# A decoder step with 32 experts: three experts fixed by number, in blocks of 96 slots

## The chip, the core and the metric

The kernel runs on one core of a Trainium2 chip. The metric is the device time of one execution in microseconds (us); several executions are timed and their median is compared. The engines are called PE (TensorE), DVE (VectorE), ACT (ScalarE), POOL (GpSimd) and SP (SyncE, which here only issues transfers). PEld is the loading of PE's weights.

## What is computed

One step of a decoder layer in float32: a prompt of 1024 tokens and 8 sampled tokens, together 1032 rows of 1024 numbers. A gated convolution and latent attention are merged and normalised, and the result h goes through a mixture of 32 SwiGLU experts. This last part is the one that the change touches:

```python
grp = argmax(softmax(h @ router_w_group + b_group))            # 4 groups
le = (h @ router_w_expert + b_expert)[experts of grp]          # 8 in a group
top_l, top_i = top_k(le, 2)                                    # two experts a token
for each expert e, for its rows x:                             # 2064 rows in all
    hid = silu(x @ w_gate[e]) * (x @ w_up[e])                  # 1024 -> 512
    y[row] += weight * (hid @ w_down[e])                       # 512 -> 1024
out = layernorm(alpha * h + y)
```

Each expert has three matrices of 2 MB. By the reference's inputs the experts 0, 1 and 2 get 28, 25 and 26 rows; the fullest expert gets 111 and the emptiest 18.

## The kernel before

The attention part and the output projection run first (to about 1100 us of the span). Then the experts run one after another, 32 blocks, one for each expert. The program's order of blocks is fixed: block n is the expert of rank `RANK[n]`. The ranks are worked out on the chip: the experts are sorted by their count of rows (lines 1488 to 1505 on PE, 2502 to 2527 on DVE), except the first `FIXED` ones, which keep rank = number (`key_f`, line 2374, gives them a key above every count). The rank decides how many slots a block has (`full`, `three`, `low` and `room`, lines 514 to 524): 128, 96, 64 or 32. What an expert has above its slots would go to extra blocks at the end (`NOVER`, run only if counts demand them; in the profile none ran).

For block n PE does, in this order: `gate_up(n)` (gate and up products, line 1568), `rows_in(n+1)` (turning the gathered rows of the next block, line 1510), `down_proj(n-1)`, `turn_hidden(n)` (line 1535). A block of 128 slots makes gate first and then up, each over the whole array (line 1515; down at 1541). A block of 64 makes gate and up side by side in the two halves of the array (lines 1520, 1521; down 1547). A block of 32 uses four quarters (lines 1528, 1553). A block of 96 is a 32 and then a 64, and both its gate and its up are finished only at its end.

In block 0 the place of a down projection is taken by `slot_tables` (line 1562): it sums the lists of rows (`blk_tok`) and weights of all blocks out of one-hot products that DVE makes (`oh_w`, `oh_blk`, lines 2580 to 2583, signal `wt_rdy`). DVE's order is written out by hand, and those products stand behind `swiglu_gate(0)`, the multiplication of block 0's gate by its sigmoid. The first `SOON` = 2 blocks get their rows from an earlier, separate table (`first_tok`), so that they can start ahead of that.

SP loads the matrices into a ring of ten places (`ring_at`, `load_matrix`, line 759). Matrix j = 3 * expert block + (0 gate, 1 up, 2 down). The table `before` says whose place each takes; SP waits until that one has been multiplied (`g_done`, `u_done`, `d_done`). The places 8 and 9, which matrices 10 and 11 take, hold the one-hot products, so these two wait for the slot tables (`ws_dve`). Matrices 0 to 5 belong to the fixed experts 0 and 1 and are loaded before the ranks are known; from matrix 6 on SP first waits for `ord_dve`, the sorted order (line 782). SP's transfers are served in the order in which they are issued. POOL gathers the rows of a block (line 903) and adds its results to `sums` in memory (line 908).

```python
            for q in range(3):
                sp.wait_ge(h_out[q], H_BASE[q] + 16 * (NT // 3))
                sp.wait_ge(ah_out[q], A_BASE[q] + 16 * (NT // 3))
            sp.wait_ge(ord_dve, 1)
...
            for n in range(SOON, NE):
                e = expert_at(n)
                for m in range(3):
                    load_matrix(3 * n + m, e)
```

Of the kernel before, what the change touches and what calls it, by code (L numbers as in the profile page):

```python
# [15 lines left out]
ALU = mybir.AluOpType  # L16
# [25 lines left out]
NE = NG * EG  # L42
# [5 lines left out]
SOON = 2  # L48
# [16 lines left out]
class Chain:  # L65
# [5 lines left out]
    def link(self, ins):  # L71
        self.n += 1
        ins.then_inc(self.sem, 1)
        self.eng.wait_ge(self.sem, self.base + self.n)
# [11 lines left out]
def build(nc, a):  # L86
    ctx = ExitStack()
    with ctx:
        def sem(name):
            return ctx.enter_context(nc.semaphore(name))  # L90
# [317 lines left out]
        ord_dve = sem("ord_dve")  # L408
# [91 lines left out]
            p, rest = divmod(n + 1, 2 * NQ)  # L500
            return NQ * p + max(0, rest - NQ)

        FIXED, FULL, MID, LOW = 2, 10, 20, 30
        kinds = {"f": iter(range(FIXED, FULL)), "m": iter(range(FULL, MID)), "h": iter(range(MID, LOW)), "q": iter(range(LOW, NE))}
        RANK = list(range(FIXED)) + [next(kinds[c]) for c in "hhfmhfmhfmhmhfmhfmhfmhfmhmfmqq"]
        assert sorted(RANK) == list(range(NE))
        def main(n):
            return P if full(n) else P // 2
# [3 lines left out]
        assert T * NE < FIRST  # L512

        def full(n):
            return RANK[n] < FULL

        def three(n):
            return FULL <= RANK[n] < MID

        def room(n):  # L520
            return P if full(n) else 3 * P // 4 if three(n) else P // 4 if low(n) else P // 2

        def low(n):
            return RANK[n] >= LOW

        def rest(n):
            return low(n) or three(n)

        def rest_at(n):
            return P // 2 if three(n) else 0  # L530
# [9 lines left out]
        def place(j):  # L540
            return place_of[j]
# [59 lines left out]
        def _(sp):  # L601
# [156 lines left out]
            def load_matrix(j, e):  # L758

                if before[j] is not None:  # L760
                    n, m = divmod(before[j], 3)
                    sp.wait_ge((g_done, u_done, d_done)[m], n + 1)
                elif place(j) >= 8:
                    sp.wait_ge(ws_dve, 1)
                sp.dma_start(ring(j), matrix(j % 3, e)).then_inc(we_ld[place(j)], 16)
# [13 lines left out]
            for q in range(3):  # L779
                sp.wait_ge(h_out[q], H_BASE[q] + 16 * (NT // 3))  # L780
                sp.wait_ge(ah_out[q], A_BASE[q] + 16 * (NT // 3))
            sp.wait_ge(ord_dve, 1)

            def expert_at(n):
                return sp.value_load(order[0:1, RANK[n]:RANK[n] + 1].bitcast(I32), min_val=0, max_val=NE - 1)

            for n in range(SOON, NE):
                e = expert_at(n)
                for m in range(3):
                    load_matrix(3 * n + m, e)  # L790
            n, m = divmod(max(j for j in range(3 * NE) if place(j) == 6), 3)
# [35 lines left out]
        def _(pool):  # L827
# [72 lines left out]
            def gather_block(table, blk, par, loaded, rows=P):  # L900

                off = bass.IndirectOffsetOnAxis(ap=table[0:rows, blk:blk + 1].bitcast(U32), axis=0)
                pool.indirect_dma_start(xg[0:rows, par, :], None, h_rows, off, bounds_check=T - 1, oob_is_err=False).then_inc(loaded, 16)
# [14 lines left out]
            for e in range(NE + 4):  # L918
                if e < NE:
# [6 lines left out]
                    else:  # L926
                        gather_block(blk_tok, RANK[e], e % 2, xg_ld[e % 2], room(e))
                if e >= 4:
# [20 lines left out]
        def _(pe):  # L949
# [615 lines left out]
            def gate_up(n):  # L1565

                pe.wait_ge(we_ld[place(3 * n)], landed(3 * n))
                pe.wait_ge(te_act, n + 1)
                pe.wait_ge(te_dve, n + 1)
                pe.wait_ge(gm_dve, n)  # L1570
                if full(n):
                    up(2, ring(3 * n), n % 2).then_inc(g_done, 1)
                    pe.wait_ge(we_ld[place(3 * n + 1)], landed(3 * n + 1))
                    pe.wait_ge(hu_dve, n)
                    up(3, ring(3 * n + 1), n % 2).then_inc(u_done, 1)
                else:
                    pe.wait_ge(we_ld[place(3 * n + 1)], landed(3 * n + 1))
                    pe.wait_ge(hu_dve, n)
                    if rest(n):
                        g, u = up_rest(ring(3 * n), ring(3 * n + 1), n % 2, rest_at(n))  # L1580
                    if not low(n):
                        g, u = up_halves(ring(3 * n), ring(3 * n + 1), n % 2)
                    g.then_inc(g_done, 1)
                    u.then_inc(u_done, 1)
# [346 lines left out]
        def _(dve):  # L1931
            chain = Chain(dve, dve_chain)
            link = chain.link
            tt, stt = nc.vector.tensor_tensor, nc.vector.scalar_tensor_tensor
# [578 lines left out]
            def width(out, by):  # L2513

                link(ts(out, by, float(FULL), None, ALU.is_lt))
                link(stt(out=out, in0=by, scalar=float(MID), in1=out, op0=ALU.is_lt, op1=ALU.add))
                link(stt(out=out, in0=by, scalar=float(LOW), in1=out, op0=ALU.is_lt, op1=ALU.add))
                link(ts(out, out, float(P // 4), float(P // 4), ALU.mult, ALU.add))
# [203 lines left out]
```

## Time and profile before

| | us |
|---|---|
| median of 3 executions | 1719.39 |
| lowest, highest | 1716.16, 1719.78 |
| the profiled execution, its own time | 1711.8 |
| its span in the trace | 1710.0 |
| PE busy in the span | 1642.7 (96%) |
| DVE, ACT, POOL busy | 661.3, 339.4, 163.9 |

The span runs from the first to the last instruction; the profiled execution took 1.8 us more than its span, and 7.6 us less than the median. Starts in the trace are us from the start of the span. A group of instructions is called by its line in the kernel. The granted clock of PE is 1.00 at 2.4 GHz and 0.50 at 1.2 GHz. The DMA share is the mean busy share of the core's 16 DMA engines.

### The profile page before, as it was taken

To read this page: it belongs to the slowest core of one execution; us is meant where nothing else is said; L and a number is where in the kernel's file an instruction comes from. 1 tells how busy PE (TensorE), PEld (TensorE's weight loads), DVE (VectorE), ACT (ScalarE), POOL (GpSimd) and SP (SyncE) were. 2 spreads that over 40 slices of the span, in tenths; PEclk is the share of its full clock that TensorE was granted. 3 is DMA by queue.
4 is the path that set the end of the run, shared out by engine and by line. 5 is a ranking of instruction groups with operands and counts; after the bars stand their busy time and mean duration, and the time that the engine had idled before them with its cause. 6 is when DMAs were issued, how large, how long until landed. Compare 5 with 4: busy or idle time off the path is not lost.

```text
span 1710.0 us, 22521 instructions
## 1 busy us (share of the span) xinstructions
PE 1642.7 (96%) x9285; PEld 1009.8 (59%) x9286; DVE 661.3 (39%) x1395; ACT 339.4 (20%) x670; POOL 163.9 (10%) x169
## 2 busy tenths in 40 slices
PE   7999999999999999999999999999999999999990
PEld 5556777777777666666688555654444444444440
DVE  1446464544542323232477745551111212121225
ACT  1113222323231221222122000101111111111115
POOL 1000000000002422111000000001111111111110
PEclk9999999999999999999999999989999999999995
DMA  7201121121027445443263443289999999999975
GB/s 229 62 18 24 50 63 50 52 61 50 13 75 210 170 148 172 140 136 112 65 235 125 187 160 136 101 302 390 391 392 377 392 395 391 381 389 396 389 268 203
DMA packets 104410, 337.67 MB, mean 197 GB/s; under 512 B 24378, under 2 KB 68482, under 8 KB 87924
## 3 DMA queue, kind: packets, MB, share of 16 engines
q1 hardware_dynamic: 89572, 276.22, 43.0%
q0 software_dynamic: 13568, 55.78, 10.8%
q10 hardware_dynamic: 1168, 4.23, 0.6%
q8 instruction: 75, 1.23, 0.3%
q14 instruction: 27, 0.22, 0.0%
HBM read 307.90 MB, written 35.51 MB: 201 GB/s over the span
## 4 chain that ended last, share of the span: by engine, by line
PE 91%; DMA 5%; DVE 2%; issue 1%; ACT 1%; POOL 0%; SPq 0%; DVEq 0%; POOLq 0%; ACTq 0%
PE psum L1075 12%; PE psum L1189 10%; PE psum L1515 8%; PE psum L1520 7%; PE psum L1377 6%; PE psum L1392 5%; PE psum L1541 4%; PE psum L1116 4%; PE psum L1547 4%; PE psum L979 3%; PE psum L1228 3%; PE psum L1089 2%; DMA arena<-in_w_up 2%; PE psum L1134 2%; PE psum L1528 2%; PE psum L1123 2%
## 5 line engine op out<-in xcount | busy, mean ns | idle before, releaser
L1075 PE MATMUL psum<-arena 128*128 128x258 f32 x896 | 215.3, 384 | 0.0
L1189 PE MATMUL psum<-arena 128*128 128x344 f32 x576 | 182.3, 458 | 0.0
L1075 PEld LDWEIGHTS psum<-arena 128*128 128x128 f32 x896 | 162.9, 190 | 27.9 <-issue 7.0
L1520 PE MATMUL psum<-arena 128*64 128x512 f32 x320 | 141.6, 595 | 0.0
L1521 PE MATMUL psum<-arena 128*64 128x512 f32 x320 | 141.6, 595 | 0.0
L1515 PE MATMUL psum<-arena 128*128 128x512 f32 x320 | 139.8, 595 | 1.1 <-DVE arena L2552 1.1
L1189 PEld LDWEIGHTS psum<-arena 128*128 128x128 f32 x576 | 103.3, 190 | 52.9 <-issue 11.2
L1515 PEld LDWEIGHTS psum<-arena 128*128 128x128 f32 x320 | 60.0, 190 | 73.6 <-issue 73.2
L1377 PE MATMUL psum<-arena 128*128 128x258 f32 x448 | 99.9, 387 | 0.9 <-ACT arena L1802 0.9
L1392 PE MATMUL psum<-arena 128*128 128x512 f32 x224 | 99.2, 596 | 0.0
L1377 PEld LDWEIGHTS psum<-arena 128*128 128x128 f32 x448 | 86.6, 194 | 14.3 <-issue 1.3
L1520 PEld LDWEIGHTS psum<-arena 128*64 128x64 f32 x320 | 42.2, 137 | 85.0 <-issue 84.1
L872 POOL DMA_INDIRECT arena<-in_cache_ckv,arena x32 | 31.0, 968 | 620.4 <-DVE arena L2091 455.1
L2184 DVE COPY arena<-psum 128x512 f32<-128x512 f32 x64 | 44.2, 691 | 113.5 <-PE psum L1228 113.2
L1547 PE MATMUL psum<-arena 128*64 128x512 f32 x320 | 73.1, 598 | 0.0
L1116 PE MATMUL psum<-arena 96*128 96x512 f32 (+3 forms) x192 | 72.2, 488 | 0.0
L1541 PE MATMUL psum<-arena 128*128 128x512 f32 x160 | 71.3, 599 | 0.0
L1392 PEld LDWEIGHTS psum<-arena 128*128 128x128 f32 x224 | 41.5, 190 | 47.4 <-issue 47.3
L1228 PE MATMUL psum<-arena 128*128 128x128 f32 x512 | 66.3, 273 | 0.0
L1756 ACT COPY arena<-psum 128x512 f32<-128x512 f32 x64 | 37.5, 585 | 144.7 <-PE psum L1228 144.7
L908 POOL DMA_INDIRECT sums<-arena x32 | 47.7, 1491 | 191.3 <-DVE arena L2629 87.8
L1228 PEld LDWEIGHTS psum<-arena 128*128 128x128 f32 x512 | 59.2, 141 | 10.1 <-issue 0.2
(394 smaller groups left out, 2125.6 us busy)
## 6 DMA issues: line engine op xcount, KB each, us to landing
arena<-in_w_gate SPq DMA_DIRECT2D x32, 2048.0 KB, 24.7
arena<-in_w_up SPq DMA_DIRECT2D x32, 2048.0 KB, 30.3
arena<-in_w_down SPq DMA_DIRECT2D x32, 2048.0 KB, 30.6
arena<-in_w_in SPq DMA_DIRECT2D x33, 512.0 KB, 5.3
gates<-arena SPq DMA_DIRECT2D x16, 516.0 KB, 6.1
arena<-gates SPq DMA_DIRECT2D x16, 516.0 KB, 6.6
arena<-in_x_prompt SPq DMA_DIRECT2D x16, 512.0 KB, 4.5
arena<-in_w_o SPq DMA_DIRECT2D x1, 4096.0 KB, 17.6
```

The lines of the kernel that those rows point to most:

```text
L979: ins = mm(psum[0:m, 3 * s + b, 0:SP3], wring[:, slot, k, 0:m], xT[:, k, b * SP3:(b + 1) * SP3], start=(k == 0), stop=(k == KD - 1))
L1075: ins = mm(psum[:, BANK[name[0]], 0:QT], held, moved, start=(k == 0 and name in ("X1", "V6", "Y5")), stop=(k == 3), skip_group_check=True)
L1116: ins = mm(psum[:, 2 * hh + b // 512, 0:w], qT[0:QK, hh, i * P:(i + 1) * P], kT[0:QK, hh, b:b + w], start=True, stop=True)
L1189: ins = mm(psum[:, FB + t, 0:SP3], wring[:, u, k, :], xT[:, k, t * SP3:(t + 1) * SP3], start=(k == 0), stop=(k == KD - 1))
L1228: ins = nc.tensor.transpose(psum[:, c, r * P:(r + 1) * P], kn[par][:, G, r0 + r, c * P:(c + 1) * P], ident)
L1377: ins = mm(psum[:, 3 * g + "XYV".index(name[0]), 0:QT], held, moved, start=(k == 0 and name in ("X1", "V6", "Y5")), stop=(k == 1), skip_gr ...
L1392: ins = mm(psum[:, 2 * (n % 2) + c, :], mT[:, k, t * P:(t + 1) * P], wo_sb[:, k, c * 512:(c + 1) * 512], start=(k == 0), stop=(k == KD - 1))
L1515: ins = mm(psum[:, bank, :], xgT[:, xpar, k, :], w[:, k, :], start=(k == 0), stop=(k == KD - 1))
L1520: g = mm(psum[0:64, 2, :], xgT[:, xpar, k, 0:64], wg[:, k, :], start=(k == 0), stop=(k == KD - 1))
L1521: u = mm(psum[64:P, 3, :], xgT[:, xpar, k, 0:64], wu[:, k, :], start=(k == 0), stop=(k == KD - 1))
L1541: ins = mm(psum[:, 5 + n, :], hhT[:, par, k, :], w[:, k, n * 512:(n + 1) * 512], start=(k == 0), stop=(k == 3))
L1547: ins = mm(psum[64 * n:64 * n + 64, 5 + n, :], hhT[:, par, k, 0:64], w[:, k, n * 512:(n + 1) * 512], start=(k == 0), stop=(k == 3))
```

## The change

The number of fixed experts goes from two to three, and the fixed ones are no longer blocks of 128 slots but of 96. Of the ranks 3 to 31, eight get 128 slots, ten 96, nine 64 and two 32; so there are now 8 blocks of 128 (before 10), 13 of 96 (before 10), 9 of 64 (before 10) and 2 of 32. The order of the blocks from block 3 on is the same as before; block 2 was a 64 and is now the fixed expert 2. Expert 2's matrices 6, 7 and 8 are loaded ahead of the wait for the order. `SOON` stays at 2, so block 2's rows still come from the slot tables. `width`, which DVE runs twice, has one instruction more.

```diff
--- before.py
+++ after.py
@@ -500,9 +500,9 @@
             p, rest = divmod(n + 1, 2 * NQ)
             return NQ * p + max(0, rest - NQ)
 
-        FIXED, FULL, MID, LOW = 2, 10, 20, 30
+        FIXED, FULL, MID, LOW = 3, 11, 21, 30
         kinds = {"f": iter(range(FIXED, FULL)), "m": iter(range(FULL, MID)), "h": iter(range(MID, LOW)), "q": iter(range(LOW, NE))}
-        RANK = list(range(FIXED)) + [next(kinds[c]) for c in "hhfmhfmhfmhmhfmhfmhfmhfmhmfmqq"]
+        RANK = list(range(FIXED)) + [next(kinds[c]) for c in "hfmhfmhfmhmhfmhfmhfmhfmhmfmqq"]
         assert sorted(RANK) == list(range(NE))
         def main(n):
             return P if full(n) else P // 2
@@ -512,10 +512,10 @@
         assert T * NE < FIRST
 
         def full(n):
-            return RANK[n] < FULL
+            return FIXED <= RANK[n] < FULL
 
         def three(n):
-            return FULL <= RANK[n] < MID
+            return RANK[n] < FIXED or FULL <= RANK[n] < MID
 
         def room(n):
             return P if full(n) else 3 * P // 4 if three(n) else P // 4 if low(n) else P // 2
@@ -779,12 +779,15 @@
             for q in range(3):
                 sp.wait_ge(h_out[q], H_BASE[q] + 16 * (NT // 3))
                 sp.wait_ge(ah_out[q], A_BASE[q] + 16 * (NT // 3))
-            sp.wait_ge(ord_dve, 1)
+            for m in range(2):
+                load_matrix(3 * SOON + m, SOON)
 
             def expert_at(n):
                 return sp.value_load(order[0:1, RANK[n]:RANK[n] + 1].bitcast(I32), min_val=0, max_val=NE - 1)
 
-            for n in range(SOON, NE):
+            load_matrix(3 * SOON + 2, SOON)
+            sp.wait_ge(ord_dve, 1)
+            for n in range(FIXED, NE):
                 e = expert_at(n)
                 for m in range(3):
                     load_matrix(3 * n + m, e)
@@ -2513,6 +2516,7 @@
             def width(out, by):
 
                 link(ts(out, by, float(FULL), None, ALU.is_lt))
+                link(stt(out=out, in0=by, scalar=float(FIXED), in1=out, op0=ALU.is_ge, op1=ALU.mult))
                 link(stt(out=out, in0=by, scalar=float(MID), in1=out, op0=ALU.is_lt, op1=ALU.add))
                 link(stt(out=out, in0=by, scalar=float(LOW), in1=out, op0=ALU.is_lt, op1=ALU.add))
                 link(ts(out, out, float(P // 4), float(P // 4), ALU.mult, ALU.add))
```

**SP, the transfers around the wait for the order.** The names are signals that the row waits for; the kernel's line 765 is one matrix. Before:

```order
L765 DMA arena<-in_w_down 128x4096 [waits h_dve,lg_done]
L785 TENSOR_LOAD arena [waits wconv_ld2,gate_out1,gate_out2,wconv_ld1,ord_dve,gate_out0,wconv_ld0]
L785 ISA x2
L765 ISA
L765 DMA arena<-in_w_gate 128x4096
L765 DMA arena<-in_w_up 128x4096
L765 DMA arena<-in_w_down 128x4096 [waits g_done]
L785 TENSOR_LOAD arena
L785 ISA x2
L765 ISA [waits u_done]
L765 DMA arena<-in_w_gate 128x4096
L765 DMA arena<-in_w_up 128x4096 [waits ws_dve]
```

After:

```order
L765 DMA arena<-in_w_down 128x4096 [waits h_dve,lg_done]
L765 DMA arena<-in_w_gate 128x4096 [waits gate_out1,wconv_ld2,wconv_ld1,gate_out2,gate_out0,wconv_ld0]
L765 DMA arena<-in_w_up 128x4096
L765 DMA arena<-in_w_down 128x4096 [waits g_done]
L786 TENSOR_LOAD arena [waits ord_dve]
L786 ISA x2
L765 ISA [waits u_done]
L765 DMA arena<-in_w_gate 128x4096
L765 DMA arena<-in_w_up 128x4096 [waits ws_dve]
L765 DMA arena<-in_w_down 128x4096 [waits ws_dve]
```

The two matrices 6 and 7 no longer stand behind `ord_dve`, and matrix 8 waits for `g_done` of block 0 as it did. Matrix 9 waits for `u_done`, matrices 10 and 11 for `ws_dve` in both.

**PE, from block 0's gate and up to the slot tables and block 1.** Before:

```order
L1515 MATMUL psum<-arena 128x512 [waits te_dve,gm_dve,te_act,we_ld0]
L1515 MATMUL psum<-arena 128x512 x7
L1515 MATMUL psum<-arena 128x512 [waits hu_dve,we_ld1]
L1515 MATMUL psum<-arena 128x512 x7
L1510 MATMUL psum<-arena 128x128 [waits xg_ld1]
L1510 MATMUL psum<-arena 128x128 x7
L1562 MATMUL psum<-arena 128x96 [waits oh_dve,wt_rdy]
L1562 MATMUL psum<-arena 128x96 x17
L1535 MATMUL psum<-arena 128x128 [waits th_act,hu_dve]
```

After, from the last products of block 0's gate and up (the lines have moved by 3: 1513, 1523, 1524, 1531, 1538 and 1565 are the old 1510, 1520, 1521, 1528, 1535 and 1562):

```order
L1523 MATMUL psum<-arena 64x512
L1524 MATMUL psum<-arena 64x512
L1513 MATMUL psum<-arena 128x96 [waits xg_ld1]
L1513 MATMUL psum<-arena 128x96 x7
L1565 MATMUL psum<-arena 128x96 [waits oh_dve,wt_rdy]
L1565 MATMUL psum<-arena 128x96 x17
L1538 MATMUL psum<-arena 128x96 [waits th_act,hu_dve]
L1538 MATMUL psum<-arena 128x96 x3
L1531 MATMUL psum<-arena 32x256 [waits gm_dve,we_ld4,te_dve,hu_dve,te_act,we_ld3]
L1531 MATMUL psum<-arena 32x256 x31
```

The 16 products of block 0 over the whole array have become 32 of the quarter form and then 8 + 8 of the half form, of which the last two stand above; the slot tables with their wait for `wt_rdy` stay behind them, and block 1 is a 96 as well. (In the trace each product is two instructions.)

**DVE, around block 0's gate.** Before:

```order
L2578 TENSOR_TENSOR arena<-arena 128x9 [waits dve_chain]
L2541 TENSOR_TENSOR arena<-arena,psum 128x512 [waits gs_act,dve_chain]
L2580 TENSOR_TENSOR arena<-arena 128x18x48
L2582 TENSOR_TENSOR arena<-arena 128x9x48 [waits dve_chain] x2
L2583 TENSOR_TENSOR arena<-arena 128x18x48 [waits dve_chain]
L2586 TENSOR_TENSOR arena<-arena 128x512
```

After (moved by 4 lines or more; 2584 to 2587 are the old 2580 to 2583):

```order
L2582 TENSOR_TENSOR arena<-arena 128x9 [waits dve_chain]
L2548 TENSOR_TENSOR arena<-arena,psum 64x256 [waits gs_act,dve_chain]
L2550 TENSOR_TENSOR arena<-arena,psum 64x512
L2584 TENSOR_TENSOR arena<-arena 128x18x48
L2586 TENSOR_TENSOR arena<-arena 128x9x48 [waits dve_chain] x2
L2587 TENSOR_TENSOR arena<-arena 128x18x48 [waits dve_chain]
L2590 TENSOR_TENSOR arena<-arena 128x512
```

The products for the slot tables stand behind the gate's multiplication (`gs_act`) in both; the one multiplication has become two.

## Rows read from the trace of the kernel before

**Rows 1.** Busy time by stretch (PE, PEld, DVE, ACT, POOL; clock, DMA share, GB/s)

```profile
1400.00:1500.00 100.00, 100.00 (x512) 43.98 (x506) 19.60 (x33) 14.07 (x28) 13.79 (x12) 1.00 1.01 391
```

**Rows 2.** Waits, 1100 to 1670 us: total us, times, longest

```profile
PE psum L1528 <- DMA arena<-in_w_up: 2.6, 2, 1.5
```

**Rows 3.** Timeline of SP: start, us, line (transfers of expert matrices)

```profile
1105.75 0.33 SPq L765 DMA_DIRECT2D arena<-in_w_down  x1
...
1115.65 0.36 SPq L765 DMA_DIRECT2D arena<-in_w_gate  x1
...
1128.82 0.33 SPq L765 DMA_DIRECT2D arena<-in_w_down  x1
...
1141.85 0.33 SPq L765 DMA_DIRECT2D arena<-in_w_up  x1
...
1626.22 0.33 SPq L765 DMA_DIRECT2D arena<-in_w_down  x1
```

**Rows 4.** DMA issues at 1128.82, 1141.85 and 1626.22 us: us to landing last

```profile
arena<-in_w_down SPq DMA_DIRECT2D x1, 2048.0 KB, 8.3
...
arena<-in_w_up SPq DMA_DIRECT2D x1, 2048.0 KB, 10.0
...
arena<-in_w_down SPq DMA_DIRECT2D x1, 2048.0 KB, 36.8
```

**Rows 5.** Chain of waits, from 1040 us: start, us, line, instructions

```profile
1118.92 1.72 PE psum L1510 x8
...
1121.69 13.97 PE psum L1515 x32
...
1136.54 4.68 PE psum L1562 x36
...
1211.10 3.59 PE psum L1528 x64
...
1221.70 1.03 PE psum L1510 x8
```

**Rows 6.** Timeline, end of a block of 96 slots

```profile
1600.71 1.16 PE L1510 MATMUL psum<-arena 128*128 128x128 f32 x8
...
1602.11 0.67 DVE L2546 TENSOR_TENSOR arena<-arena,psum 64x512 f32<-64x512 f32 x1
```

**Rows 7.** Timeline of DVE, the products for the slot tables

```profile
1130.13 1.05 DVE L2580 TENSOR_TENSOR arena<-arena 128x864 f32<-128x864 f32 x1
...
1132.51 1.06 DVE L2583 TENSOR_TENSOR arena<-arena 128x864 f32<-128x864 f32 x1
```

**Rows 8.** Instructions by line and shape, 1100 to 1710 us: busy us, mean ns

```profile
L1541 PE MATMUL psum<-arena 128*128 128x512 f32 x160 | 71.3, 599 | 0.0
...
L1547 PE MATMUL psum<-arena 128*64 128x512 f32 x320 | 73.1, 598 | 0.0
...
L1553 PE MATMUL psum<-arena 128*32 128x256 f32 x384 | 23.2, 382 | 0.6 <-ACT arena L1849 0.6
```

**Rows 9.** Busy time by stretch, as rows 1 (clock third from the end); PE's last products

```profile
1100.00:1104.00 4.00, 3.15 (x14) 2.43 (x14) 2.47 (x6) 1.87 (x2) 0.00 (x0) 0.57 0.44 179
...
1110.00:1122.00 12.00, 9.32 (x28) 5.73 (x28) 5.49 (x26) 1.58 (x3) 2.01 (x2) 0.57 0.75 273
...
1668.00:1672.00 4.00, 0.00 (x0) 0.00 (x0) 0.47 (x2) 1.87 (x3) 1.34 (x1) 0.79 0.21 29
...
1664.54 1.93 PE L1553 MATMUL psum<-arena 128*32 128x256 f32 x32 [0.60 <-ACT arena L1849]
```

**Rows 10.** Gathers: POOL's timeline; DMA issues at 1111.27 and 1602.65 us

```profile
1111.27 1.03 POOL L903 DMA_INDIRECT arena<-h_rows,arena  x1 [4.04 <-DVE arena L2508]
...
arena<-h_rows,arena POOLq DMA_INDIRECT x1, 3.3
...
arena<-h_rows,arena POOLq DMA_INDIRECT x1, 7.3
```

## The prediction

> **What bounds the kernel now.** I read the busy time by stretch first. Between 1400 and 1500 us PE is busy all the time, at a granted clock of 1.00, and so are the DMA engines, with a share of 1.01 at 391 GB/s [rows 1]. Two resources are full, so the next view is who waits. PE waited for a matrix of an expert only twice, 2.6 us in all [rows 2]: it looks like a kernel bound by PE. The landings say otherwise. Matrix 10 was issued at 1141.85 us [rows 3] and landed 10.0 us later [rows 4], at 1151.85; the last one, matrix 95, was issued at 1626.22 and landed 36.8 us later, at 1663.0. The queue in front of the transfers grew from one matrix to six. The 85 matrices between the two landings took 511.2 us, 6.01 us each, without a gap. So from about 1150 us on the transfers are the bound, PE runs just behind them, and the 2.6 us are where it touched them. A PE that has less to do would wait more, and the end would stay. What moves the end is **when the stream of transfers gets going**, at 1140 us.
>
> What holds it back there is the ring: matrix 8 waits for block 0's gate, matrix 9 for its up, matrices 10 and 11 for the slot tables. Matrix 8 was issued at 1128.82 [rows 3], at half time of block 0's gate and up, which took 13.97 us from 1121.69 on [rows 5]; matrix 10 at 1141.85, 0.63 us after the tables' end at 1136.54 + 4.68 = 1141.22.
>
> **The change, part by part.**
>
> 1. *Fewer slots.* A block of 128 costs PE 13.97 us for gate and up [rows 5] and 71.3 / 10 = 7.13 us for down [rows 8]. A block of 96 costs 1221.70 - 1211.10 = 10.60 us [rows 5] and 73.1 / 20 + 23.2 / 12 = 5.59 us [rows 8], a saving of 4.91. The old block of 64 cost 10.60 - 3.59 = 7.01 and 3.66 us, so block 2 grows by 5.52. Together PE saves 2 x 4.91 - 5.52 = 4.3 us. By the first paragraph the end gains nothing from it. The rows that gathers and additions move are the experts' real ones and stay 2064, so the transfers carry the same bytes.
>
> 2. *Expert 2's matrices earlier.* Matrix 6 was issued at 1115.65, behind the order; it now goes out behind matrix 5, issued at 1105.75 [rows 3]. Matrix 5 takes until about 1114, and two more at under 6 us each are in at about 1125. Then the queue is empty, because matrix 8 still waits for block 0's gate and matrix 10 for the tables. Nobody needs 6 and 7 before block 2, at about 1161. Gain: 0. It would be worth something only if the ring had a free place.
>
> 3. *The slot tables come later.* This is the term that counts. In a block of 96 the gate is finished only with the up, 10.60 us after its start: at 1121.69 + 10.60 = 1132.29, where it used to be done at half time, about 1128.7. DVE multiplies it by its sigmoid and then makes the products for the tables; that is its written order. In a block of 96 DVE is through with the gate 1602.11 + 0.67 - 1600.71 = 2.07 us after PE turned to the next rows [rows 6], here at 1134.36. The products for the tables took from 1130.13 to 1132.51 + 1.06 = 1133.57, 3.44 us [rows 7], so they will be ready at 1137.80. PE has turned block 1's rows by then (1.03 us [rows 5], to 1133.3) and **stands still for 4.5 us**, which it did not do before: the gate in the first half of 13.97 us hid all of DVE's work. The tables end at 1137.80 + 4.68 = 1142.48, which is 1.26 us later than before. Matrix 10 is issued 1.3 us later, at 1143.1. Matrices 8 and 9 go out together at about 1132.4 and are in by about 1147 (8.3 us for the one [rows 4], 6.01 for the next), so they neither delay nor help it by more than some tenths. The stream starts **1.3 us later** and stays so to the end. Of PE's 4.3 us 3.37 are block 0's gate and up and already in this; the other 0.9 come back by block 3. So PE ends 0.3 us late and the transfers 1.3: the transfers decide.
>
> 4. *PE's clock after the stall.* The trace has no stall like this amid full work, so I bound it. At the end of the program the last product was through at 1664.54 + 1.93 = 1666.5, and the clock went from full (2.4 GHz) to half (1.2 GHz) at 1670.3, which is the 0.79 between 1668 and 1672 [rows 9]: after 3.8 us of rest. The stall of 4.5 us is longer, so the likeliest is a fall just as the tables start. How long it stays down: both the 4 us from 1100 on and the 12 us from 1110 on have a mean of 0.57, which is 3.4 us and 10.3 us at half [rows 9]. At half level work takes about double (eight turns 1.72 us [rows 5] against 1.03), so the loss is 1.7 or 5.2 us; no fall at all is 0. I take 1.7, since the tables and block 1 are dense work, unlike the work in the long stretch. It falls on the tables' end and so on matrix 10: **+1.7 us**.
>    The Trainium skill (TensorE: Matmul & The Clock Gate, HAM oscillation) has waits of 3 to 5 us throttle the clock every time, with about 1.67 us spent at half level after each. By that the loss would be 0.8 us as an estimate and the time 1721.5; the trace disagrees about the length, since its shortest low stretch is 3.4 us.
>
> 5. *The rest.* One more instruction in `width` on the way to PE's start in block 0: under 0.2 us, made up by the smaller copy of 96 slots. The gather of block 0 was issued at 1111.27 and took 3.3 us [rows 10] beside a half-empty queue; now matrices 6 and 7 are in it. Between full transfers a gather of 24 rows took 7.3 us [rows 10], which would be 1118.6, and PE turned the rows at 1118.92 [rows 5]. It just fits: 0, at worst a few us. The further tail behind PE's last product shifts with it.
>    The Trainium skill (DMA: Bandwidth & Descriptors, Queues, rings and completion order) says that each DMA engine alternates between its queues packet by packet. By that the gather is slowed by the weights, not put behind them, which the 7.3 us agree with.
>
> Sum: 1.3 + 1.7 = +3.0 us. The profiled execution would go from 1711.8 to 1714.8; it lies 7.6 us under the median, so I add the 3.0 to the median of 1719.39: **1722.4 us**. A measurement of this kernel can tell about 0.2% (3.4 us) from no change, so this is just inside.
>
> **The rivals.**
>
> *A. The clock does not fall* (20%). For it: 3.8 us of rest passed at full level [rows 9], and the stall is only 0.7 longer. Then only the 1.3 remain: 1720.7 us.
>
> *B. The clock stays low over the tables and most of block 1* (25%). This ends on the slower side. Place: the stall of 4.5 us before the tables. Price: the long stretch, half of 10.3 us, gives 1.3 + 5.2 = 6.5, so 1725.9 us. It decides for slower from 2.1 us of loss on, which is 4.2 us at half level. For it: of the two low stretches one was that long, and the eight turns at 1118.92, late in it, still ran low [rows 5]. Against it: the other was over in 3.4 us.
>
> *C. The early transfers do help* (7%). If the stream is not tied to the tables, because the queue before matrix 10 is what limits it, then the two matrices that land some 4 us earlier and PE's 4.3 us count: 1719.4 - 4.0 = 1715.4 us. Against it: matrix 10 landed 10.0 us after its issue, hardly more than matrix 8 with 8.3 behind an empty queue [rows 4], so it was its own issue that set it.
>
> *D. Block 0's gather comes late* (6%). If it takes as long as matrix 10, 10.0 us [rows 4], it lands at 1121.3, 2.4 us after PE wants it, and all of block 0 shifts: 1722.4 + 2.4 = 1724.8 us.
>
> *E. An extra block runs* (2%). With more than 96 rows for expert 0, 1 or 2, a block of 21 us of PE's work with three unhidden matrices and gather comes on top, some 60 us: 1780 us. By the reference these experts have 28, 25 and 26 rows, and then the change does just what it says.
>
> **How the numbers follow.** The forecast has 40%, A 20, B 25, C 7, D 6, E 2. The likeliest case gives 1722.4. The range goes from 1717.0, between C and A with the spread of the runs before, to 1727.0, which takes in B and D; it leaves out most of C, E and the far end of B. Faster by over 0.2% is C: 0.07. Of the forecast a good third may land beyond 3.4 us by the spread of the runs; with B and D that makes slower 0.45, and 0.48 is left for within 0.2%.
>
> **What would show it.** Right: PE waits about 4.5 us for DVE before the slot tables (the wait for `wt_rdy`); matrix 6 is issued near 1106 and matrix 10 about 1.3 to 3 us later than before; the granted clock dips after 1137; matrices land 6.0 us apart from there on, and PE's waits for expert matrices grow beyond 2.6 us or stay. Wrong: no such wait before the tables, a last matrix that lands earlier than 1663.0, or intervals between landings that are shorter than 6.0 us, which would mean that the transfers were not the bound.

## The result and the profile after

| | before | after |
|---|---|---|
| median | 1718.64 us of 4 runs | 1727.66 us of 4 runs |
| lowest, highest | 1716.16, 1719.78 | 1726.29, 1729.7 |
| profiled execution, its span | 1711.8, 1710.0 | 1727.33, 1725.4 |

The ratio is 1.0059, with a 95% interval of 1.0043 to 1.0075: **9.0 us slower**. The forecast was 1722.4, with a range up to 1727.0. The direction of the sum was right, its size was not. The later samples of the kernel before, of 18 to 35 executions on other chips, have medians of 1715.05 to 1716.34 us (only the eight of e10 have 1718.11), so the 1718.64 of these four may be high and the 9.0 us too small; e9 below has 14.6. Two executions of the kernel before that fell far out of the rest, at 9683 and 4384 us, count in no ratio.

The router ahead of the experts ran 2.0 us later in this execution already. So I count from the last product of line 1421 (1424 after), which starts at 1100.94 us before and at 1102.94 after. PE's timeline of the changed kernel, around block 0 (start, us, line; in brackets the idle time before and what ended it):

```profile
1122.88 1.55 PE L1513 MATMUL psum<-arena 96*128 96x96 f32 x8 [1.72 <-DMA arena<-h_rows,arena]
1125.30 5.72 PE L1531 MATMUL psum<-arena 128*32 128x256 f32 x64 [0.87 <-ACT arena L1845]
...
1137.97 1.13 PE L1513 MATMUL psum<-arena 96*128 96x96 f32 x8
1143.56 8.72 PE L1565 MATMUL psum<-arena 8*128 8x96 f32 x36 [4.46 <-DVE arena L2587]
1152.08 0.85 PE L1538 MATMUL psum<-arena 96*128 96x96 f32 x4
1152.85 4.14 PE L1531 MATMUL psum<-arena 128*32 128x256 f32 x64
```

The predicted stall is there, 4.46 us before the slot tables. But the tables behind it took 8.72 us instead of 4.75 (4.68 in the chain of [rows 5]), and block 0's turning waited 1.72 us for its gather. DVE's timeline shows where the stall comes from, as forecast, in the written order:

```profile
1139.03 0.41 DVE L2548 TENSOR_TENSOR arena<-arena,psum 64x256 f32<-64x256 f32 x1 [6.37 <-ACT arena L1849]
...
1142.45 1.06 DVE L2587 TENSOR_TENSOR arena<-arena 128x864 f32<-128x864 f32 x1
```

Busy time by stretch, with the clock third from the end, then the DMA share and GB/s:

```profile
1114.00:1128.00 14.00, 9.57 (x49) 5.41 (x52) 7.58 (x31) 1.76 (x2) 1.23 (x2) 0.50 0.83 330
...
1128.00:1138.00 10.00, 10.00 (x77) 3.68 (x69) 4.38 (x15) 0.00 (x0) 0.00 (x0) 0.92 0.00 0
...
1142.00:1144.00 2.00, 0.44 (x2) 0.44 (x2) 1.97 (x3) 0.00 (x0) 0.00 (x0) 0.79 0.99 414
1144.00:1152.00 8.00, 8.00 (x36) 7.49 (x36) 3.30 (x8) 0.00 (x0) 0.00 (x0) 0.50 0.72 307
1152.00:1154.00 2.00, 2.00 (x22) 1.26 (x25) 1.54 (x9) 0.48 (x1) 0.39 (x1) 0.65 0.29 49
```

PE rested from 1139.10. The level is either full or half, so the 0.79 puts the fall to half level 1.16 us into its stretch, at 1143.2, after 4.1 us of rest; the 0.65 puts the rise 1.4 us into its own, at 1153.4. That is 10.2 us at half, the tables wholly in it. An earlier low stretch holds on past 1128: the 0.92 between 1128 and 1138 is 1.6 us at half, so it ends at 1129.6, 4.3 us into block 0's products. And the transfers lay idle for 10 us, from 1128 to 1138. SP's timeline shows why:

```profile
1107.70 0.33 SPq L765 DMA_DIRECT2D arena<-in_w_down  x1
1108.26 0.33 SPq L765 DMA_DIRECT2D arena<-in_w_gate  x1
1108.64 0.42 SPq L765 DMA_DIRECT2D arena<-in_w_up  x1
1138.06 0.33 SPq L765 DMA_DIRECT2D arena<-in_w_down  x1
1139.78 0.36 SPq L765 DMA_DIRECT2D arena<-in_w_gate  x1
1152.91 0.34 SPq L765 DMA_DIRECT2D arena<-in_w_up  x1
...
1641.95 0.33 SPq L765 DMA_DIRECT2D arena<-in_w_down  x1
```

These are the matrices 5 to 10 and 95. Matrix 8 comes 35.1 us after the reference point, before 27.9 [rows 3], and matrix 10 comes 50.0 after it, before 40.9: **9.1 us late**. The gather of block 0 in POOL's timeline, and its DMA issue with the us to landing:

```profile
1113.27 1.00 POOL L906 DMA_INDIRECT arena<-h_rows,arena  x1 [4.02 <-DVE arena L2511]
...
arena<-h_rows,arena POOLq DMA_INDIRECT x1, 9.6
```

Before it was 3.3 [rows 10]. PE's waits for expert matrices (total, times, longest) went from 2.6 [rows 2] to 6.2 us:

```profile
PE psum L1531 <- DMA arena<-in_w_up: 6.2, 4, 2.5
```

So more of the end belongs to the transfers, not less.

### The profile page after: what moved, and what is told of

Same layout as the page of the kernel before. It is cut to its first block, busy times and chain, and to the rows that moved or that the text cites. A ratio compares the mean times of both kernels' runs of the same rounds, so it can differ in the third digit from the quotient of the medians.

```text
span 1725.4 us, 23117 instructions
## 1 busy us (share of the span) xinstructions
PE 1651.4 (96%) x9573; PEld 1015.9 (59%) x9574; DVE 668.2 (39%) x1413; ACT 342.6 (20%) x679; POOL 162.4 (9%) x169
## 2 busy tenths in 40 slices
DMA packets 104348, 337.71 MB, mean 196 GB/s; under 512 B 24314, under 2 KB 68418, under 8 KB 87860
## 4 chain that ended last, share of the span: by engine, by line
PE 86%; DMA 9%; DVE 3%; issue 1%; ACT 1%; SPq 0%; POOL 0%; DVEq 0%; POOLq 0%; ACTq 0%
PE psum L1078 12%; PE psum L1192 10%; PE psum L1523 7%; PE psum L1380 6%; PE psum L1518 6%; PE psum L1395 5%; DMA arena<-in_w_up 5%; PE psum L1119 4%; PE psum L1550 4%; PE psum L982 3%; PE psum L1231 3%; PE psum L1092 2%; PE psum L1544 2%; PE psum L1531 2%; PE psum L1137 2%; PE psum L1126 2%
## 5 line engine op out<-in xcount | busy, mean ns | idle before, releaser
L1078 PEld LDWEIGHTS psum<-arena 128*128 128x128 f32 x896 | 162.8, 190 | 27.9 <-issue 7.0
L1524 PE MATMUL psum<-arena 128*64 128x512 f32 x352 | 155.8, 595 | 0.0
L1523 PE MATMUL psum<-arena 128*64 128x512 f32 x352 | 155.8, 595 | 0.0
L1192 PEld LDWEIGHTS psum<-arena 128*128 128x128 f32 x576 | 104.1, 191 | 53.8 <-issue 12.7
L1518 PE MATMUL psum<-arena 128*128 128x512 f32 x256 | 111.9, 595 | 0.0
L1523 PEld LDWEIGHTS psum<-arena 128*64 128x64 f32 x352 | 46.4, 137 | 94.1 <-issue 93.3
L1395 PE MATMUL psum<-arena 128*128 128x512 f32 x224 | 99.2, 595 | 0.0
L1380 PEld LDWEIGHTS psum<-arena 128*128 128x128 f32 x448 | 86.6, 194 | 14.3 <-issue 1.3
L1518 PEld LDWEIGHTS psum<-arena 128*128 128x128 f32 x256 | 48.0, 190 | 57.9 <-issue 57.4
L1550 PE MATMUL psum<-arena 128*64 128x512 f32 x352 | 80.4, 598 | 0.0
L1395 PEld LDWEIGHTS psum<-arena 128*128 128x128 f32 x224 | 41.5, 190 | 47.4 <-issue 47.3
L1531 PE MATMUL psum<-arena 128*32 128x256 f32 x960 | 60.8, 409 | 7.1 <-DMA arena<-in_w_up 6.2
L2548 DVE TENSOR_TENSOR arena<-arena,psum 64x256 f32<-64x256 f32 x15 | 6.2, 415 | 155.2 <-ACT arena L1849 144.8
```

The source lines that it names most:

```text
L1078: ins = mm(psum[:, BANK[name[0]], 0:QT], held, moved, start=(k == 0 and name in ("X1", "V6", "Y5")), stop=(k == 3), skip_group_check=True)
L1192: ins = mm(psum[:, FB + t, 0:SP3], wring[:, u, k, :], xT[:, k, t * SP3:(t + 1) * SP3], start=(k == 0), stop=(k == KD - 1))
L1380: ins = mm(psum[:, 3 * g + "XYV".index(name[0]), 0:QT], held, moved, start=(k == 0 and name in ("X1", "V6", "Y5")), stop=(k == 1), skip_gr ...
L1395: ins = mm(psum[:, 2 * (n % 2) + c, :], mT[:, k, t * P:(t + 1) * P], wo_sb[:, k, c * 512:(c + 1) * 512], start=(k == 0), stop=(k == KD - 1))
L1518: ins = mm(psum[:, bank, :], xgT[:, xpar, k, :], w[:, k, :], start=(k == 0), stop=(k == KD - 1))
L1523: g = mm(psum[0:64, 2, :], xgT[:, xpar, k, 0:64], wg[:, k, :], start=(k == 0), stop=(k == KD - 1))
```

## The experiments

Every experiment starts from the kernel after or the kernel before, as said, and computes the same outputs; the filling products of three of them are read by nobody. The table has, in us from the reference point, when PE starts to turn block 0's rows, when SP issues matrices 8 and 10, how long the slot tables take, and the start of the final load of `sums`. Those are from the one profile of each; the ratio is timed, against the kernel before on the same chip. The runs e1 to e4 shared one chip, e5 to e8 a second and e9 to e12 a third. The kernel before took in the median 1716.34, 1715.05 and 1715.52 us on them, and differences of ratios between chips are less sure: each has some 0.2% either way.

| | block 0 | m8 | tables | m10 | final | ratio (95%) |
|---|---|---|---|---|---|---|
| before | 17.8 | 27.9 | 4.7 | 40.9 | 576.2 | |
| after | 19.9 | 35.1 | 8.7 | 50.0 | 589.6 | 1.0059 (1.0043-1.0075) |
| e1_late_loads | 22.5 | 35.2 | 8.7 | 50.0 | 590.1 | 1.0058 (1.0040-1.0076) |
| e2_tables_first | 20.1 | 35.3 | 4.7 | 41.8 | 584.0 | 1.0051 (1.0032-1.0070) |
| e3_both | 22.5 | 35.3 | 4.7 | 41.8 | 583.2 | 1.0019 (1.0003-1.0035) |
| e4_warm_stall | 24.7 | 38.7 | 4.7 | 49.5 | 587.3 | 1.0061 (1.0043-1.0080) |
| e5_block0_full | 22.5 | 31.9 | 4.7 | 44.9 | 582.0 | 1.0021 (1.0009-1.0033) |
| e6_early_only | 21.0 | 32.7 | 4.7 | 45.8 | 579.1 | 1.0025 (1.0011-1.0039) |
| e7_less_pe_work | 22.4 | 31.7 | 4.7 | 44.8 | 581.1 | 1.0006 (0.9994-1.0017) |
| e8_half_blocks_first | 22.6 | 31.5 | 7.6 | 43.5 | 579.7 | 0.9986 (0.9973-1.0000) |
| e9_changed_again | 24.7 | 38.8 | 8.7 | 53.7 | 592.8 | 1.0085 (1.0070-1.0100) |
| e10_before_again | 17.8 | 27.9 | 4.7 | 40.9 | 577.9 | 1.0005 (0.9989-1.0022) |
| e11_late_and_warm | 22.5 | 35.2 | 4.7 | 46.1 | 586.3 | 1.0038 (1.0025-1.0052) |
| e12_half_and_warm | 17.6 | 26.5 | 4.7 | 35.7 | 571.0 | 0.9981 (0.9968-0.9993) |

The first column falls into two groups, near 17.8 and 22.5 where the gather is not slowed, and near 20 (21.0 in e6) and 24.7 where it is. What separates 17.8 from 22.5 is the clock over the router, which came to full level for some us in the one and stayed at half in the other. Busy time by stretch, e1_late_loads, where the 0.57 is half level but for some 4 us at the two ends (from 1100 to 1123 it is 0.50 throughout):

```profile
1096.00:1124.00 28.00, 25.41 (x109) 19.91 (x107) 13.71 (x55) 2.33 (x4) 3.77 (x3) 0.57 0.49 172
```

and e10_before_again:

```profile
1109.00:1116.00 7.00, 6.40 (x40) 4.54 (x39) 3.57 (x21) 0.26 (x1) 1.96 (x2) 0.94 0.74 266
```

Profiles of both kinds occur with and without the change, and both with the unaltered changed kernel (after and e9). That nothing but the clock makes the difference is a reading of the rows. So the one profile is read from block 0's start on, or compared with one of the same kind, and what a part costs in all goes by the timed ratios. 0.1% of the table is 1.7 us.

**e1: the early transfers alone undone** (from the kernel after).

```diff
+            sp.wait_ge(ord_dve, 1)
             for m in range(2):
                 load_matrix(3 * SOON + m, SOON)
...
-            sp.wait_ge(ord_dve, 1)
             for n in range(FIXED, NE):
```

> The changed kernel with matrices 6, 7 and 8 of expert 2 put back behind the wait for the order; everything else as changed. Theory S (the end follows the start of the stream of transfers, that is the issue of matrix 10 after the slot tables, one to one; the early transfers only delayed the gather of block 0 by 1.7 us and left PE's clock at half level 2.1 us' worth longer): matrix 10 is issued 3.7 us earlier counted from the last turning of rows ahead of the router, time 1724.0 us against 1727.7 of the changed kernel; PE's stall of 4.5 us before the tables and the tables at half clock (8.7 us) stay. Rival C (the early transfers helped or cost nothing, and the loss is all in the stall): 1727.7 us or above.

1726.86 us. The gather is quick again:

```profile
arena<-h_rows,arena POOLq DMA_INDIRECT x1, 3.7
```

but this router ran at half level, so block 0 did not start earlier than in the profile after and the expected 1724.0 us did not come. Against e9, whose router ran so too, matrix 10 goes out 3.7 us earlier. The ratio is that of the first measurement of the kernel after and 0.27% under that of e9, both on other chips: by itself it does not settle the price of the early transfers. Stall and slow tables are the same as after.

**e2: the products for the tables ahead of block 0's gate on DVE** (from the kernel after).

```diff
-            swiglu_gate(0)
...
+            swiglu_gate(0)
```

> The changed kernel with DVE's four products for the slot tables moved ahead of the multiplication of block 0's gate. Theory S: the products are ready before PE wants them, the stall of 4.5 us goes, the clock does not fall, the tables take 4.7 us instead of 8.7: matrix 10 is issued 8.5 us earlier and the time is 1719.2 us. Rival P (PE's total work and not the start of the stream sets the end, the stall is made up later by waits that shrink): the time gains less than 4 us, above 1723.7.

1724.99 us, 5.8 more than expected. The stall is gone and the tables are fast:

```profile
1122.91 1.54 PE L1513 MATMUL psum<-arena 96*128 96x96 f32 x8 [1.98 <-DMA arena<-h_rows,arena]
...
1139.05 4.75 PE L1565 MATMUL psum<-arena 8*128 8x96 f32 x36
```

Matrix 10 went out 8.2 us earlier than after, and the final load only 5.6. The wait for the gather stays, and block 0's first products are as slow as after (5.71 us).

**e3: both edits.**

> Both edits: expert 2's matrices behind the order, and the products for the tables ahead of the gate. Theory S: 1727.7 - 3.7 - 8.5 = 1715.5 us; that is 3.2 us below the kernel before, by the 3.4 us that a block of 96 takes less than one of 128 in front of the tables. Rival (the transfers are full from elsewhere on and an earlier start of the stream below the old one gives nothing): 1718.6 us as before the change.

1719.78 us, 4.3 more than expected. Two comparisons on one chip and in the same rounds follow. e3 against e1: 0.39%, **6.7 us**, for stall and slow tables together. e3 against e2: 0.32%, **5.5 us**, for the early transfers. Both are clear of noise, though not sharp: drawing the executions anew gives 4.6 to 8.4 us for the first and 1.5 to 6.5 for the second. 3.3 us over the kernel before are left.

**e4: PE kept busy through the stall** (from the kernel after). `keep_busy` is the kernel's own helper for filling products; here 4.1 us of them.

```diff
+                keep_busy(6, 5)
                 pe.wait_ge(wt_rdy, 1)
```

> The changed kernel with six products of 384 columns that nobody reads (ident by constants, into a free bank) put in front of the wait for the products of the tables, so that PE works through most of its stall of 4.5 us. Theory S: the wait for DVE stays as long in all, but the clock does not fall, the tables take 4.7 us instead of 8.7, matrix 10 is issued 4.0 us earlier: 1723.7 us. Rival (the clock's fall costs nothing, as the stream of transfers does not hang on the tables): 1727.7 us or slightly above.

1726.45 us instead of 1723.7, which by itself does not show the gain. The tables took 4.75 us, as expected. Between block 0's start and the final load lie 562.6 us, in the profiles after and e9 569.6 and 568.1; but block 0 started at 24.7. In e9, of the same kind, matrix 10 goes out 4.1 us later and the ratio is 0.24% higher; the first measurement of the kernel after has the same ratio as e4. I repeated it without the early transfers (e11).

**e5: e3 with block 0 at 128 slots**, so that its gate is done at half time again and matrix 8 goes out earlier.

```diff
         def full(n):
-            return FIXED <= RANK[n] < FULL
+            return n == 0 or FIXED <= RANK[n] < FULL
...
         def three(n):
-            return RANK[n] < FIXED or FULL <= RANK[n] < MID
+            return 0 < n < FIXED or FULL <= RANK[n] < MID
```

> As e3_both, but block 0 computed as a block of 128 again (blocks 1 and 2 stay 96). Theory M (after the tables are dealt with, what is left of the loss is matrix 8: it waits for block 0's gate, which in a block of 96 is finished only with the up; the transfers stand idle until then): matrix 8 is issued at half time of block 0 again, some 4 us earlier than in e3_both, and the time falls from 1719.8 us to the 1716.3 of the kernel before. Rival (the width of block 0 does not matter, the loss of e3_both lies in the width's extra work or in blocks 1 and 2): 1719.8 us.

1718.84 us, ratio 1.0021: no better than e3 (1.0019). Matrix 8 is 3.4 us earlier and matrix 10 3.1 later, since block 0 is longer. That the two cancel is a guess: no run moves matrix 8 alone.

**e6: the early transfers alone**, with the experts 0 and 1 at 128 slots and expert 2 at 64.

```diff
-            return FIXED <= RANK[n] < FULL
+            return RANK[n] < 2 or FIXED <= RANK[n] < FULL
...
-            return RANK[n] < FIXED or FULL <= RANK[n] < MID
+            return FULL <= RANK[n] < MID
...
-                link(stt(out=out, in0=by, scalar=float(FIXED), in1=out, op0=ALU.is_ge, op1=ALU.mult))
+                link(stt(out=out, in0=by, scalar=2.0, in1=out, op0=ALU.not_equal, op1=ALU.mult))
```

> The early transfers alone: expert 2 fixed, its matrices 6 to 8 ahead of the order, but experts 0 and 1 in blocks of 128 and expert 2 in one of 64, so that PE's work per block is that of the kernel before. Theory S: no gain from the head start; the gather of block 0 lands 9.6 us after its issue instead of 3.3, block 0 starts some 2 us later, everything behind it too: 1718 to 1719 us against 1716.3 of the kernel before. Rival C (a head start for two matrices fills idle transfers and shortens the stream): below 1716.3 us, down to 1712.

1719.4 us, 4.3 over the kernel before; expected were 1.7 to 2.7. The gather took 10.3 us, and PE waits 3.30 us for it. The clock had come back to full level before, fell during this wait, and gate and up of block 0 took 15.59 us instead of 13.97:

```profile
1123.64 1.97 PE L1513 MATMUL psum<-arena 128*128 128x128 f32 x8 [3.30 <-DMA arena<-h_rows,arena]
1126.67 15.59 PE L1518 MATMUL psum<-arena 128*128 128x512 f32 x32 [1.05 <-DVE arena L2556]
```

Matrix 10 goes out 4.9 us later than before the change (45.8 against 40.9), which is the 4.3 us of the timed runs within their noise. So the early transfers alone make this kernel slower, and nothing of them comes back.

**e7: four of the full blocks at 96 slots** (from the kernel before), some 4 x 4.91 = 19.6 us less of PE's work and nothing else.

```diff
-        FIXED, FULL, MID, LOW = 2, 10, 20, 30
+        FIXED, FULL, MID, LOW = 2, 6, 20, 30
...
-        RANK = list(range(FIXED)) + [next(kinds[c]) for c in "hhfmhfmhfmhmhfmhfmhfmhfmhmfmqq"]
+        RANK = list(range(FIXED)) + [next(kinds[c]) for c in "hhfmhmmhfmhmhmmhfmhmmhfmhmmmqq"]
```

> The kernel before with four of its eight sorted blocks of 128 turned into blocks of 96 (the experts in them have at most 94 rows, so nothing spills): PE has 4 x 4.9 = 19.6 us less to do, well behind the start of the stream. Theory S (the transfers bound the experts' part): PE's waits for matrices grow by about that much and the time stays at 1716.3 us, within 2. Rival P (PE's work bounds it): 1697 us.

1716.62 us, the time of the kernel before (ratio 1.0006, at most 1.0017). Of the 19.6 us of work, 14.2 show as longer waits for matrices, 16.8 in place of 2.6:

```profile
PE psum L1528 <- DMA arena<-in_w_up: 16.8, 8, 3.4
```

PE's work saved behind the start of the stream is worth nothing, so the transfers bound the experts' part.

**e8: experts 0 and 1 at 64 slots, and the products for the tables first** (from the kernel before).

```diff
         def full(n):
-            return RANK[n] < FULL
+            return FIXED <= RANK[n] < FULL
...
                 link(stt(out=out, in0=by, scalar=float(MID), in1=out, op0=ALU.is_lt, op1=ALU.add))
+                link(stt(out=out, in0=by, scalar=float(FIXED), in1=out, op0=ALU.is_ge, op1=ALU.mult))
...
-            swiglu_gate(0)
...
+            swiglu_gate(0)
```

> The kernel before with its two fixed experts in blocks of 64 and DVE's products for the tables ahead of block 0's gate. Theory S and M: gate and up of block 0 are both finished after 7.0 us, matrix 8 is issued as before and matrix 9 seven us earlier, the tables end about 4 us earlier and matrices 10 and 11 with them: the stream starts some 3 to 4 us earlier and the time is 1712.5 us against 1716.3. Rival (the stream's start is not what counts): 1716.3 us.

1713.4 us, ratio 0.9986; the interval, 0.9973 to 1.0000, just reaches no change. DVE is now late for the shorter block, and PE stands still for 2.78 us. The clock fell all the same, at 1139.2 (the 0.58 in the stretch from 1139 to 1140, third from the end), 1.3 us after PE had gone back to work, and the tables are slow:

```profile
1137.82 7.61 PE L1562 MATMUL psum<-arena 8*128 8x96 f32 x36 [2.78 <-DVE arena L2583]
...
1139.00:1140.00 1.00, 1.00 (x8) 1.00 (x7) 0.93 (x3) 0.00 (x0) 0.00 (x0) 0.58 0.95 410
```

**e9 and e10: the kernels after and before once more**, unaltered.

> The changed kernel once more, unaltered, to have it on the same chip and in the same rounds as the others and with a second profile. Theory S and T (T: in most executions PE's clock stays at half through the whole router part, as in five of the six profiles of variants without or with the early transfers; then the gather of block 0 is issued later and the early transfers still delay its landing, so block 0 starts another 2 us later than in the first profile): 1726 to 1728 us, and in the profile matrix 8 is issued 35 to 38.6 us and matrix 10 50 to 53 us after the last turning of rows begins. Rival (the first four runs were by chance slow): below 1723 us.

> The kernel before once more, for a second profile. Theory T: the first profile of it was a lucky one, in which the clock was back at full level during the router. An ordinary one starts block 0's rows 22.4 us after the last turning begins (not 17.8), issues matrix 10 at 44.8 (not 40.9) and takes 1714 to 1717 us. Rival (the first profile was typical): 17.8 and 40.9.

e9: 1729.57 us; on this chip the change costs 0.85%, 14.6 us, on the first one 0.59%. The gather took 10.5 us and the stall was 4.47. As in e6 the clock had come back to full level, here at 1123.6, when the wait for the gather began, and fell again behind it, at 1127.0; block 0's first products took 5.09 us:

```profile
1125.46 1.13 PE L1513 MATMUL psum<-arena 96*128 96x96 f32 x8 [1.96 <-DMA arena<-h_rows,arena]
1127.46 5.09 PE L1531 MATMUL psum<-arena 128*32 128x256 f32 x64 [0.87 <-ACT arena L1845]
...
1145.10 8.72 PE L1565 MATMUL psum<-arena 8*128 8x96 f32 x36 [4.47 <-DVE arena L2587]
```

e10: 1718.11 us, ratio 1.0005, no difference from the runs of the kernel before beside it. Its profile repeats the events of the first one within 0.1 us up to matrix 10, so that profile was no exception and my theory T about it was wrong.

**e11: e1 and e4 together.**

> The changed kernel with expert 2's matrices behind the order (as e1) and with the six filling products before the tables (as e4). In e4 the tables took 4.75 us as expected but block 0 started 3.5 us later than in e1, so the gain did not show. Theory S: here both hold, block 0's matrix 8 is issued at 35.2 us as in e1, the tables take 4.75 us, matrix 10 is issued at 46 and not at 50 us: 1723 us against 1726.9 of e1. Rival (the clock's fall costs nothing): 1726.9 us.

1722.35 us, which was about what I expected. The stall is filled and the tables run at full level:

```profile
1139.58 4.06 PE L1402 MATMUL psum<-arena 128*128 128x384 f32 x12
1144.21 4.75 PE L1566 MATMUL psum<-arena 8*128 8x96 f32 x36 [0.57 <-DVE arena L2588]
```

In the profile matrix 10 goes out 3.9 us earlier than in e1, and the way from block 0's start to the final load is 3.8 us shorter (563.8 against 567.6): this is the price of the clock alone. The timed runs agree but do not prove it by themselves. Against e1 the ratio is 0.20% lower, **3.4 us**, across two chips, with an interval that just reaches nothing; e4 against e9, across chips as well, has 0.24%. On its own chip e11 is 0.47% faster than e9, 8.1 us for the clock and the early transfers together.

**e12: e8 with `keep_busy(4, 5)`** ahead of the wait for `wt_rdy`.

> As e8, with four filling products before the wait for the tables' products; in e8 PE stood still 2.9 us there, the clock fell and the tables took 7.6 us. Theory S: tables 4.75 us, matrix 10 issued 2.8 us earlier than in e8, at 40.7 us: 1710.6 us against 1713.4 of e8 and 1715.1 of the kernel before. Rival (matrices 8 and 9 already fill the transfers until then): 1713.4 us.

1712.81 us, ratio 0.9981 (0.9968 to 0.9993): faster than both kernels, by 3.3 us against before; the interval reaches from 5.5 us to 1.2. The gain is less than the 4.5 us expected.

```profile
1132.09 2.85 PE L1399 MATMUL psum<-arena 128*128 128x384 f32 x8
1134.94 4.75 PE L1563 MATMUL psum<-arena 8*128 8x96 f32 x36
```

Matrix 10 goes out at 35.7 us, 5.2 before that of the kernel before. Counted from block 0's start, the tables begin 5.0 us earlier than there in e8 and e12 alike, by the blocks of 64 and DVE's order, and the filling takes 2.9 us off the tables. In time it is worth little over e8 (0.05%, within the intervals).

## Why the prediction was wrong

The time from the reference point to the end of the tables, term by term, in the two profiles:

| | forecast | measured |
|---|---|---|
| start of block 0 (step 5) | 0 | +2.2 |
| block 0's turning, gate and up (step 3) | -3.4 | -1.7 |
| turning block 1 and the stall (step 3) | +4.6 | +4.6 |
| the tables' own time (step 4) | +1.7 | +4.0 |
| end of the tables | +3.0 | +9.1 |

- **Step 1 held.** Fewer slots bring nothing. e7 shows it with a saving over four times as large. The bytes stayed as forecast too, 337.67 MB before and 337.71 after.
- **Step 2 was half right.** Nothing was gained by the early matrices. That they could cost something I looked for in step 5 only, and there I took it for nothing.
- **Step 3 held**: 4.46 us against 4.5. DVE's order and the gate that is done only with the up make the stall, and e2 and e3 remove it. Of matrices 8 and 9 I said that they neither delay nor help. Matrix 8 was late by 7.2 us and the engines lay idle for 10. An earlier matrix 8 at the price of a longer block brought nothing in e5; an earlier one alone was not tried.
- **Step 4 failed**, with 2.3 of the 6.1 us that the sum lacks. The fall was forecast rightly, its length was not. I took the short low stretch of [rows 9], 3.4 us, and argued that the tables are dense work. It was 10.2 us, as long as the long one of 10.3, and the tables lost 4.0 us, not 1.7. Rival B had this mechanism, and its 1725.9 was the nearest number. Its bound of 5.2 us held the measured one, though the low stretch covered the tables and only the first half us of block 1's gate and up. The profile of e11 against e1 has the size with one edit, at 3.9 us. I read density as a reason for a quick rise, and no row supported that: almost 10 us of full work at half level stand between the fall and the rise. Rival A's ground, that 3.8 us of rest had passed at full level, was no safe bound either: in e8 a rest of 2.78 us was followed by a fall.
- **Step 5 failed by more**, with 3.8 of the 6.1 us. The gather of block 0 took 9.6 us, not the 7.3 that I carried over from the middle of the kernel. "It just fits" left no room, and 2.3 us more became 1.72 us of waiting; DVE's one more instruction in `width`, taken for nothing, is 0.2 of the rest. The low clock then lasted 4.3 us into block 0, whose first products took 5.72 us instead of 3.66: this is the half of the saving that is missing in step 3. I had treated the end of that low stretch as given. But all five profiles with early transfers have a slow start of block 0 (5.72, 5.71, 4.90 and 5.09 us for those products in after, e2, e4 and e9; 15.59 for 13.97 in e6), and none of the others has (3.66 in e1, e3 and e11, 13.97 in e5, e7 and e10). So the slow start comes with the wait for the gather and is a second part of its price. Rival D had the place of this right, with 2.4 us and 6%. B and D came true together, and the prediction had no case for that.
- **The rule on the queues** was weighed in step 5. The gather, issued at 1113.27 with matrix 5 under way and 6 and 7 waiting, landed at about 1122.9; matrix 7 was in at 1128.2. It is slowed by them and not put behind them. The Trainium skill (DMA: Bandwidth & Descriptors, Queues, rings and completion order) has a DMA engine take packets from its queues in turn; this order of landing fits it, but no price of the gather follows from it.
- **The rule on the clock.** The stretch at half level behind the stall was 10.2 us. The Trainium skill (TensorE: Matmul & The Clock Gate, HAM oscillation) has a wait of 3 to 5 us throttle the clock, which happened here, and about 1.67 us at half level after it, with which the trace disagrees.

The forecast's own measure, the stream's start, explains 9.1 us. The final load was 13.4 us later in the profile, and 4.3 us of that came after the tables: the 81 intervals from matrix 12's landing to matrix 93's took 491.6 us against 486.4, or 6.07 each against 6.00. What makes them longer is open, but it goes with the number of blocks of 96 slots and not with the early transfers: with ten such blocks they took 485.6 to 487.4 us (before, e6, e8, e10), with twelve to fourteen 489.4 to 491.6 (after, e1, e2, e3, e4, e5, e7). This would be most of the 0.2% by which e3 and e5 stay over the kernel before. e7 has 489.4 as well, and in its time no more than 0.06% shows, so the step from these intervals to the time is not shown.

The early transfers are the cause that the forecast lacked. Their price in time is 5.5 us by e2 against e3, on one chip, and 4.3 by e6. The pairs across chips, e9 against e1 and e4 against e11, give 4.6 and 4.0, each alone hardly clear of noise. Profiles of the same kind give the same: with them matrix 10 goes out 3.4 to 4.9 us later (45.8 against 40.9, 53.7 against 50.0, 49.5 against 46.1), some 2 to 3 us of it by the start of block 0 and the rest by its slow products. Only the first measurement of the kernel after, beside e1, shows nothing of it. Stall and clock (6.7 us), early transfers (5.5) and what is left in e3 (3.3) add up to 15.5 us. That is near the 14.6 of e9 and above the 9.0 of the first four runs.

## What to carry to other kernels

A stall inside dense work is not priced by its own length: if the clock may fall, price it with the longest low stretch that the trace shows, and look what runs in it. A load that is moved ahead of everything is not free because nobody waits for it; ask which small, urgent transfer shares the engines with it, and what PE's clock does while PE waits for that one. When one engine's block gets shorter, check the written order of the engine that it hid: here four products of DVE moved ahead of a multiplication gave back 6.7 us.

## What the runs showed of the hardware

- A rest of 4.1 us in full work brought PE's clock to half level for 10.2 us, and the tables behind it took 8.72 us against 4.75. In e1 the level was half from 1140.2 (a mean of 0.62 from 1140 to 1141) to 1153.9 (0.55 from 1153 to 1154), 13.7 us, behind the same stall.
- In e8 PE rested 2.78 us only. The clock fell 1.3 us after it had gone back to work and was low for 10.2 us too, and the tables took 7.61 us.
- With matrices 5, 6 and 7 issued ahead of it, the gather of 28 rows took 9.6 to 10.5 us (five profiles); with matrix 5 alone 2.9 to 3.8 (seven profiles).
- The changed kernel, unaltered, started block 0 in one profile 19.9 us and in another 24.7 us after the reference point, and the kernel before and e7, which differ only in later blocks, 17.8 and 22.4. In each pair the router's clock differed. In the runs beside e9 to e12 the kernel before took from 1710.22 to 1723.89 us.
